# Gates of a PEER layer added to a table in device memory by indirect DMAs and multiplied in tile by tile on GpSimd

## What is computed

```python
def block(x_t):
    q = jnp.einsum('td,dhk->thk', x_t, w_q).reshape(T, PEER_HEADS, 2, PEER_HALF)
    s = jnp.einsum('thpk,hpnk->thpn', q, sub_keys).astype(jnp.float32)
    sv, si = lax.top_k(s, K)
    cand = (sv[:, :, 0, :, None] + sv[:, :, 1, None, :]).reshape(T, PEER_HEADS, K * K)
    cidx = (si[:, :, 0, :, None] * PEER_NKEYS + si[:, :, 1, None, :]).reshape(T, PEER_HEADS, K * K)
    fv, fpos = lax.top_k(cand, K)
    eidx = jnp.take_along_axis(cidx, fpos, axis=-1)
    gate = jax.nn.softmax(fv, axis=-1)
    u = u_emb[eidx]
    v = v_emb[eidx]
    act = jax.nn.gelu(jnp.einsum('thkd,td->thk', u, x_t).astype(jnp.float32), approximate=False)
    return jnp.einsum('thk,thkd->td', (gate * act).astype(x_t.dtype), v)
```

## Time and profile before

| | |
|---|---|
| median of three runs | 2896.46 us |
| profiled execution: time, span | 2905.77 us, 2904.0 us |
| busy in the span: PE, DVE, ACT, POOL | 91%, 64%, 46%, 1% |
| DMA | 446.96 MB, mean 154 GB/s |
| mean granted TensorE clock | 0.965 of full speed |
| weighing, each of two | about 108 us from the key stage's last Gelu to the value stage's first matmul |

### The profile page before, as it was taken

The page is one execution under the profiler, slowest core; times in us unless marked ns, Lnnn a source line. Parts: engine busy times, 40 slices in busy tenths (PEclk is TensorE's granted clock), DMA queues, the critical chain, the costliest instruction groups (busy, mean ns, idle before and its releaser), DMA issues. The chain is left out here.

```text
span 2904.0 us, 48556 instructions
## 1 busy us (share of the span) xinstructions
PE 2656.2 (91%) x17804; PEld 2386.7 (82%) x17804; DVE 1872.3 (64%) x3595; ACT 1341.5 (46%) x2044; POOL 38.5 (1%) x62
## 2 busy tenths in 40 slices
PE   5789999998999999699999998999999779888989
PEld 4689999987888878399999987888879558687978
DVE  6767888688666664555787579555554455553654
ACT  3344444566454553444455566455454220254343
POOL 0000000000000001000000000000000200000000
PEclk9899999999999999799999999999999898999999
DMA  8446666711777754054565520666645300242545
GB/s 337 154 156 188 218 223 218 229 66 32 236 238 240 245 157 144 1 159 140 184 182 181 182 86 3 194 194 192 192 151 166 102 8 1 67 140 92 164 137 155
DMA packets 122549, 446.96 MB, mean 154 GB/s; under 512 B 13360, under 2 KB 13872, under 8 KB 121808
## 3 DMA queue, kind: packets, MB, share of 16 engines
q1 hardware_dynamic: 114096, 415.22, 44.8%
q10 hardware_dynamic: 8352, 30.51, 2.8%
HBM read 444.63 MB, written 1.05 MB: 153 GB/s over the span
## 5 line engine op out<-in xcount | busy, mean ns | idle before, releaser
L267 DVE TENSOR_TENSOR weight_low<-weight_raw,weight_high 128x1024 fp32r<-128x1024 f32 x732 | 892.5, 1221 | 445.9 <-ACT weight_high L261 442.2
L395 PE MATMUL bank<-h_high,weight_high 128*128 128x256 f32 x3552 | 1019.0, 287 | 78.2 <-DVE weight_low L267 20.8
L261 ACT ACTIVATE weight_high<-weight_raw 128x1024 fp32r<-128x1024 f32 x732 | 773.7, 1059 | 677.8 <-DMA weight_raw<-peer_v_dram 338.7
L395 PE MATMUL bank<-h_low,weight_high 128*128 128x256 f32 x3552 | 1014.3, 286 | 0.0
L395 PE MATMUL bank<-h_high,weight_low 128*128 128x256 f32 x3552 | 1014.1, 286 | 0.0
L395 PEld LDWEIGHTS bank<-h_high,weight_high 128*128 128x128 f32 x3552 | 691.9, 195 | 94.1 <-issue 78.7
L395 PEld LDWEIGHTS bank<-h_low,weight_high 128*128 128x128 f32 x3552 | 691.9, 195 | 0.0
L395 PEld LDWEIGHTS bank<-h_high,weight_low 128*128 128x128 f32 x3552 | 691.3, 195 | 0.0
L1284 PE MATMUL bank<-weight_high,act_high 128*128 128x512 f32 x1024 | 317.5, 391 | 9.4 <-DVE weight_low L267 9.3
L1284 PE MATMUL bank<-weight_low,act_high 128*128 128x512 f32 x1024 | 316.7, 391 | 0.0
L1284 PE MATMUL bank<-weight_high,act_low 128*128 128x512 f32 x1024 | 316.4, 390 | 0.0
(11 more groups left out here) (321 smaller groups left out, 2399.9 us busy)
## 6 DMA issues: line engine op xcount, KB each, us to landing
weight_raw<-peer_u_dram SPq DMA_DIRECT2D x256, 512.0 KB, 3.5
weight_raw<-peer_v_dram SPq DMA_DIRECT2D x256, 512.0 KB, 3.5
later_modulations<-ada_later_dram ACTq DMA_DIRECT2D x54, 512.0 KB, 4.2
weight_raw<-peer_w_q_dram SPq DMA_DIRECT2D x32, 512.0 KB, 3.5
weight_raw<-w_in_dram SPq DMA_DIRECT2D x32, 512.0 KB, 3.5
weight_raw<-mlp_w_up_dram SPq DMA_DIRECT2D x32, 512.0 KB, 3.5
weight_raw<-mlp_w_down_dram SPq DMA_DIRECT2D x32, 512.0 KB, 3.5
arena<-ada_first_dram SPq DMA_DIRECT2D x6, 2048.0 KB, 21.5
```

What stands on the lines that cost most here:

```text
L261: self.nc.scalar.activation(self.high[:, slot, :], self.raw[:, slot, :], ACT.Identity) \
L267: eng.tensor_tensor(self.low[:, slot, :], self.raw[:, slot, :], self.high[:, slot, :].bitcast(F32), ALU.subtract) \
L395: mm = self.nc.tensor.matmul(out, w, x, start=(start and i == 0), stop=(stop and i == 2), skip_group_check=skip)
```

## The change

The weighing step is gone. Instead there is a table per layer in device memory with one float32 for each pair of expert and token (128 x 128 x 256 elements, 16.8 MB).

- **Clearing.** Each table is set to zero by eight DMAs of 2 MB from a row of zeros in SBUF, issued from ACT's queue: layer 0's in `even_mixer` between the second Gelu and the square root, layer 1's in `rope` of the odd mixer. GpSimd writes the zeros first.
- **Picks.** A 17th step per head computes the element's number, expert * 256 + token, as an integer (`pick_spot`). The steps are spread over 92 tiles in layer 0 and 76 in layer 1 instead of 104. Exp runs per head on ACT three tiles after the head's last step, and DVE normalizes the head's gates three tiles after that.
- **Scattering.** When a head's gates are ready, GpSimd issues 32 indirect DMAs. Each takes one gate from each of the 128 partitions and adds it to the table element that `pick_spot` names. Each element is a packet of four bytes. Between heads GpSimd waits until the head before has landed in full. That is 256 such DMAs per layer.
- **Hand-over.** SP waits for all of them before it loads the first value tile, which also needs the first tile of gates. ACT and DVE prepare the first three value tiles at the end of the key stage, and DVE weighs the first two tiles of activations.
- **Value stage.** SP loads a tile of gates (128 x 256, 128 KB, rows of 1 KB) for every value tile, two tiles ahead. GpSimd multiplies it into `acts` (126 tiles), and ACT waits for that before it rounds the tile.

```diff
+        self.expert = sb("pick_expert", [P, TT, TOPK])
+        self.spot = sb("pick_spot", [P, HEADS, TT, TOPK], U32)
...
+        self.gates = sb("gate_tiles", [P, RING, T])
+        self.table = [nc.dram_tensor(f"gate_table{layer}", (P * P * T, 1), F32, kind="Internal").ap() for layer in range(2)]
...
+CLEARINGS = 8
+
+def clear_table(core, eng, layer):
+
+    cleared, zeros = core.sig("table_cleared"), core.later[:, 0, :].unsqueeze(1).to_broadcast([P, P * T // D // CLEARINGS, D])
+    table = core.table[layer].rearrange("(p c n w) o -> c p n (w o)", p=P, c=CLEARINGS, w=D)
+    eng.wait_ge(core.sig("zeros_made").sem, layer + 1)
+    for c in range(CLEARINGS):
+        eng.dma_start(table[c], zeros).then_inc(cleared.sem, 16)
...
             nc.scalar.activation(v, v, ACT.Gelu).then_inc(gelus.sem, 1)
             nc.scalar.activation(u, u, ACT.Gelu)
+            clear_table(core, act, 0)
             act.wait_ge(vars_.sem, vars_.at(1))
             nc.scalar.activation(root, var, ACT.Sqrt, bias=core.c("eps"), scale=1.0 / 512).then_inc(rooted.sem, 1)
...
-PICK_STEPS = 16
-PICKED_BY = 104
-GATED_BY = 120
+PICK_STEPS = 17
+PICKED_BY = (92, 76)
+
+
+def picked_at(layer, h):
+
+    return max(RING - 1, ((h + 1) * PICK_STEPS - 1) * PICKED_BY[layer] // (HEADS * PICK_STEPS) + 1)
...
+        of_head = slice(h * TOPK, (h + 1) * TOPK)
+        link(nc.vector.scalar_tensor_tensor(out=b.expert[:], in0=b.chosen[:, 0, :, of_head], scalar=float(P),
+                                            in1=b.chosen[:, 1, :, of_head], op0=ALU.mult, op1=ALU.add))
+        link(nc.vector.scalar_tensor_tensor(out=b.expert[:], in0=b.expert[:], scalar=float(T),
+                                            in1=core.c("token").unsqueeze(2).to_broadcast([P, TT, TOPK]), op0=ALU.mult, op1=ALU.add))
+        nc.vector.tensor_copy(b.spot[:, h], b.expert[:]).then_inc(core.sig("experts_picked").sem, 1)
+        yield
+
+
+def load_gates(core, sp, layer, n):
+
+    slot = n % RING
+    if n >= RING:
+        weighed = core.sig("acts_weighed")
+        sp.wait_ge(weighed.sem, weighed.at(n - RING + 1))
+    sp.dma_start(core.gates[:, slot, :], core.table[layer].rearrange("(f s t) o -> f s (t o)", f=P, t=T)[n]) \
+        .then_inc(core.sig(f"gates{slot}_loaded").sem, 16)
+
+
+def weigh(core, eng, acts, n):
+
+    slot, loaded = n % RING, core.sig(f"gates{n % RING}_loaded")
+    eng.wait_ge(loaded.sem, loaded.at(16 * (n // RING + 1)))
+    eng.tensor_tensor(acts[:, n, :], acts[:, n, :], core.gates[:, slot, :], ALU.mult) \
+        .then_inc(core.sig("acts_weighed").sem, 1)
+
+
+SCATTERS = HEADS * TOPK * TT
+WEIGHED_EARLY = 2
...
         def _(sp):
             if layer == 0:
+                sp.wait_ge(cleared.sem, 16 * CLEARINGS)
                 for n in range(EARLY_MODS, EARLY_MODS + 2):
                     load_later_modulation(core, sp, n)
-            core.stream(sp, seg, k)
+            with sp.Fori(1, P // RING) as g:
+                for slot in range(RING):
+                    core.load_tile(sp, seg, g * RING + slot, slot)
+            sp.wait_ge(scattered.sem, scattered.at(16 * SCATTERS))
+            for n in range(RING):
+                if n < RING - 1:
+                    load_gates(core, sp, layer, n)
+                core.load_tile(sp, following, n, n)
+            load_gates(core, sp, layer, RING - 1)
...
         @block.scalar
         def _(act):
...
+            for n in range(P):
+                act.wait_ge(used.sem, seg.first + RING + n + 1)
+                nc.scalar.activation(acts[:, n, :], core.bank[n % RING][:, 0:T], ACT.Gelu).then_inc(free.sem, 1)
+                ahead = n + RING - 1
+                if ahead < P:
+                    core.make_high(act, seg, ahead - ahead % RING, ahead % RING)
+                else:
+                    core.make_high(act, following, 0, ahead - P)
+                if ahead in exp_at:
+                    h = exp_at[ahead]
+                    act.wait_ge(picked.sem, picked.at(h + 1))
+                    nc.scalar.activation(gates(h), gates(h), ACT.Exp).then_inc(exped.sem, 1)
...
+        @block.gpsimd
+        def _(pool):
+            pool.wait_ge(cleared.sem, 16 * CLEARINGS * (layer + 1))
+            for h in range(HEADS):
+                pool.wait_ge(gated.sem, gated.at(h + 1))
+                if h:
+
+                    pool.wait_ge(scattered.sem, scattered.at(16 * TOPK * TT * h))
+                for i in range(TOPK):
+                    for t in range(TT):
+                        pool.indirect_dma_start(core.table[layer], bass.IndirectOffsetOnAxis(ap=b.spot[:, h, t, i:i + 1], axis=0),
+                                                b.expo[:, t, h, i:i + 1], None, compute_op=ALU.add).then_inc(scattered.sem, 16)
...
+                if n in gate_at:
+                    h = gate_at[n]
+                    total = b.total[:, h * TT:(h + 1) * TT]
+                    dve.wait_ge(exped.sem, exped.at(h + 1))
+                    link(nc.vector.tensor_reduce(total, gates(h), AX_X, ALU.add))
+                    link(nc.vector.reciprocal(total, total))
+                    nc.vector.tensor_tensor(gates(h), gates(h), total.unsqueeze(2).to_broadcast([P, TT, TOPK]), ALU.mult) \
+                        .then_inc(gated.sem, 1)
+                while done < HEADS * PICK_STEPS and done * PICKED_BY[layer] < n * HEADS * PICK_STEPS:
...
+            for n in range(RING - 1):
+                core.make_low(dve, following, 0, n)
+                if n < WEIGHED_EARLY:
+                    dve.wait_ge(free.sem, free.at(n + 1))
+                    weigh(core, dve, acts, n)
...
-def peer_weigh(core, layer):
...
+            for n in range(RING, P):
+                if n == RING:
+                    load_gates(core, sp, layer, n)
+                    load_gates(core, sp, layer, n + 1)
+                if n + 2 < P:
+                    load_gates(core, sp, layer, n + 2)
+                core.load_tile(sp, seg, n, n % RING)
+            core.first_tiles(sp, k + 1)
...
+        @block.gpsimd
+        def _(pool):
+            for n in range(WEIGHED_EARLY, P):
+                weigh(core, pool, acts, n)
...
+            for n in range(P):
+                if n >= ahead:
+                    act.wait_ge(used.sem, seg.first + RING + n - ahead + 1)
+                    core.make_high(act, seg, n - n % RING, n % RING)
+                act.wait_ge(weighed.sem, weighed.at(n + 1))
+                nc.scalar.activation(core.act_high[:, n % RING, :], acts[:, n, :], ACT.Identity).then_inc(rounded.sem, 1)
...
+        if clearing:
+            @block.scalar
+            def _(act):
+                clear_table(core, act, 1)
+
         @block.gpsimd
         def _(pool):
+            if clearing:
+                nc.gpsimd.memset(core.later[:, 0, :], 0.0).then_inc(sig("zeros_made").sem, 1)
```

203 lines of the change are left out of this document (32 added, 171 removed).

## The result

The changed kernel takes **3297.69 us** (median of 4 runs, 3289.34 to 3301.09) against 2899.57 us before: a ratio of 1.137, 95% interval 1.134 to 1.140. The prediction said 2748 with a range of 2690 to 3000. The profiled execution of the changed kernel has a span of 3299.1 us.

A forecast was written before the change was run, and what follows sets the result against it. The DVE-bound weighing was taken to lie on the path between key and value stages, which go at PE's pace. 2905.8 - 208.4 + 14 + 34 + 12 = 2757.4, on the runs' scale (9.3 lower) 2748 us; range 2690 to 3000.

The forecast's parts named there:

- What bounds the kernel, and what the removal gives: Between key and value stage: the DVE-bound weighing is wholly on the path; removing it saves 104.2 us per layer, together 208.4.
- The scatters: GpSimd's 256 indirect DMAs per layer, beside the key stage: they end 4.3 and 5.7 us late, + 14 in all.
- the price x: GpSimd's time for one scatter, unknown from the trace: between 0.33 and 2.1 us, taken as 1.2.
- The first rival: GpSimd becomes the bound, PE idles at the key stage's end: 3055 us at 1.8 us per scatter, chance 0.24.
- break-even of 1.49 us: The price of one scatter above which the changed kernel would be slower than the kernel before, 2896.5 us.
- Clearing: ACT held by issuing the table's zeroing, in `even_mixer` and `rope`: + 21 and + 13, together + 34 us, from 0 to 58.
- DVE and ACT in the key stage: Key stage: DVE just fits under PE's pace; Exp's table loads and full DVE cost + 12 us, from 0 to 48.
- Value stage: DVE's splitting, GpSimd's gate product and the gate tiles' loads all fit beside PE's 2.72 us per tile: + 0.
- Full blocking: Rival in layer 0's value stage: DVE's and GpSimd's instructions run one after the other, + 17 us, 2765; chance 0.05.
- DMA engines as the bound: Rival in the key stage: four-byte packets exceed the engines' idle 60 ns each; at 0.1 us per element 2911; chance 0.05.

The follow-up runs named there:

- experiment 6: The changed kernel with each layer's scatters held until the last key tile is used, then beside loads, DVE subtractions, DVE copies and nothing in turn; 3962.3 us.
- experiment 5: The changed kernel with scatters that write (copy) the gate instead of adding it; 2958.5 us, ratio 1.020.
- experiment 1: The changed kernel without all 512 scatters and the waits on them; 2736.9 us, ratio 0.943.
- experiment 2: The changed kernel with half of the scatters left out, 16 per head instead of 32; 2763.6 us, ratio 0.952.

## Why the prediction was wrong

- **What bounds the kernel, and what the removal gives: right.** Without scatters PE waits 4.31 us at the seam, 4.2 were predicted; the weighing's 104.2 us per layer went.
- **The scatters: the step that failed.** It is the price x between an issue by SP, 0.33 us, and a landing, 2.1, of which I took "the middle", 1.2. In its own definition (without one landing of 2.1 per head) x was (606.7 - 16.8) / 256 = 2.30 us in layer 0 and (597.2 - 16.8) / 256 = 2.27 in layer 1: above my upper bound. 512 * (2.29 - 1.2) = 558 us covers the miss of 546.9 in the account's third line (177.1 + 175.4 + 2 * 97.2). The bound was wrong, and not only the choice in it. It took a landing as the worst case for one DMA, but the instruction (1.55), the gap to the next (0.30) and the pauses (0.32 per scatter) add up, and DVE lengthens the first, the loads the second (experiment 6). The premise that none waits within a head was wrong as well: GpSimd pauses after every seventh scatter. The start of the scatters was right: 271 plus the clearing's 25.8 is 297, measured 297.4.
- **The first rival is what happened**: GpSimd became the bound, SP's queue held by its wait, PE idle at the seam. It had 0.24 and a price of 1.8 us. Its break-even of 1.49 us agrees with the run nearest to it: in its definition copies cost (732.1 - 296.4 - 16.8) / 256 = 1.64 (layer 0, first scatter to SP's first load), which by the prediction's 51 us for 0.1 makes 2748 + 512 * 0.44 = 2973, and 2959 were measured, above the kernel before as it says. The reason that I gave against it, the 0.33 us of an issue in hardware, said nothing about a scatter: the profile lists the scatters' queue as software_dynamic (q0) and that of SP's loads as hardware_dynamic (q1), and a scatter keeps GpSimd busy for 1.55 us where SP's first issue of a gate tile takes 0.34; the one that I gave for it, "added, not copied", is by experiment 5 worth 2.37 - 1.70 = 0.67 us of the 1.09 by which the price exceeded mine.
- **Clearing: right, + 34 predicted.** The eight issues held ACT, and DVE's reciprocal, which started at 103.75, waited for the root:

```profile
85.21 2.80 ACTq L673 DMA_DIRECT2D gate_table<-later_modulations  x3
88.05 35.95 ACTq L673 DMA_DIRECT2D gate_table<-later_modulations  x5
...
125.90 1.75 DVE L892 RECIPROCAL work<-work 128x256 f32<-128x256 f32 x1 [22.83 <-ACT work L866]
```

  ACT was free at 124.0, where 125 was said. The account has + 25.8 for + 21, and for + 13 it has 15.1 - 2.6 = + 12.5, the value stage's part taken off.
- **DVE and ACT in the key stage: sized too high, and the near match is luck.** 8.3 us were measured against 12, but 5.0 of them are the scatters' own (experiment 1), for which the prediction had nothing. Without scatters the key stages are 1.5 us longer than before in each layer, 3 together. In layer 0 PE waited 8.2 us for DVE's low parts in eleven places between 300 and 620 us, and 4.7 in eight places in experiment 1. Each Exp has its two table loads of 1.28 us, but only 0.23 us of its own.
- **Value stage: right.** It takes 354.2 instead of 351.6 us in layer 0 and 350.2 instead of 350.1 in layer 1. The groups of layer 0, to be read against the earlier trace rows:

```profile
L268 DVE TENSOR_TENSOR weight_low<-weight_raw,weight_high 128x1024 fp32r<-128x1024 f32 x125 | 152.8, 1222 | 0.0
L1094 POOL TENSOR_TENSOR arena<-arena,gate_tiles 128x256 f32<-128x256 f32 x125 | 121.0, 969 | 219.1 <-DMA gate_tiles<-gate_table 219.1
L1306 DVE TENSOR_TENSOR act_low<-arena,act_high 128x256 fp32r<-128x256 f32 x128 | 60.8, 476 | 115.0 <-ACT act_high L1286 114.7
```

  The long low part did not slow at all (1218 to 1222 ns), the short one by 51 ns. Full blocking would have cost 17 us by the prediction's sum, and 2.6 were lost.
- **DMA engines as the bound: no.** The prediction's limit of 60 ns was for an element. The additions took 0.062 * 16 * 3299 us = 3273 us of the engines, which is 44 ns for each of the 73728 packets but 50 for each of the 65536 elements, so the margin is small. With half of the scatters beside it the key stage of layer 0 has a share of 0.74.
- The last line of the account, - 6.5 us in a stretch that the change does not touch, is no larger than what executions differ by: the same stretch takes 1079.3 us in experiment 2 and 1091.0 in experiment 5. The profiled execution of before is 9.3 us above the median of its runs.

## What to carry to other kernels

An operation that no row shows needs a price from parts that can add up (the instruction, the gap to the next, the pauses between runs of them, what runs beside it); the middle between two far rows is no estimate where 512 of them lie on one queue, and a break-even price (here 1.49 us) should have been weighed against that sum. Before work is moved to many small indirect DMAs, time one of them in the form that the kernel needs: in this kernel an addition cost 0.6 us more than a copy, and half of the elements saved only a tenth of the instruction. Look also at what it does to the stage beside it: the cheaper copies made the key stages 48 and 60 us longer. GpSimd's idle time is better used beside a bounding DVE, in the share at which the next engine becomes the bound: a quarter of the one-hots gave 1% here, a half gave nothing.

## What the runs showed of the hardware that I had not expected

- A scatter of 128 elements of 4 bytes holds GpSimd for 1.55 us as an addition and 0.96 as a copy; with 64 elements the addition takes 1.40. The next follows 0.30 us later.
- An addition of 128 elements is 144 packets, a copy 32, for the same bytes.
- Of such additions at most 3, 7 and 22 follow each other without a pause with a `dynamic_dma_scratch_size` of 1024, 2048 and 6144 bytes; the pause is some 2 us alone and 3.3 to 4.8 beside loads of 239 GB/s, and it comes after every seventh also where all before it have landed.
- Scattered copies of 4-byte elements slowed the key stage of layer 1 beside them from 361.4 to 421.4 us; with additions it took 361.6.
- DVE lengthens GpSimd's scatter from 1.55 us to 2.21 (subtractions with two SBUF inputs) or 1.88 (copies), and loads of 239 GB/s leave it at 1.55.
- GpSimd issues three stores of 2 MB one after the other in 2.47 us, and then pauses for 16 to 27 us.
